# First products of three feed-forwards: seven half-size products of operand sums in place of eight

## What is computed

```python
def _swiglu(h, w_in, w_out):
    gu = h @ w_in
    return (jax.nn.silu(gu[..., :FFN_HIDDEN]) * gu[..., FFN_HIDDEN:]) @ w_out
```

## Time and profile before

| | us |
|---|---|
| three runs | 3299.5, 3304.2, 3306.3 |
| median | 3304.2 |
| span of the profiled execution (no other time is given for it) | 3302.2 |
| PE busy in it | 3203.2 |
| DVE busy | 1573.5 |
| ACT busy | 1129.4 |
| POOL busy | 417.1 |

### The profile page before, as it was taken

One profiled execution on the slowest core, in us unless ns is written; L12 is line 12 of the kernel. 1 busy time (PEld: TensorE's weight loads), 2 busy tenths in 40 slices (PEclk: granted clock), 3 DMA queues, 4 the chain that ended last, 5 costly groups with the idle time before them and its releaser, 6 DMA issues.

```text
span 3302.2 us, 45048 instructions
## 1 busy us (share of the span) xinstructions
PE 3203.2 (97%) x19414; PEld 2595.4 (79%) x19414; DVE 1573.5 (48%) x2498; ACT 1129.4 (34%) x1827; POOL 417.1 (13%) x622
## 2 busy tenths in 40 slices
PE   7999999999999999999999999999999999989999
PEld 5787888887887888887875677888887876668886
DVE  4646454446434654444246545343344437454544
ACT  6565532124434522223245443111112336431222
POOL 1302110002200300000010015000001311030000
PEclk9999999999999999999999999999999999999999
DMA  3111123223227322232243340222202222013221
GB/s 135 53 52 53 52 83 121 77 77 118 77 102 281 103 90 77 96 108 62 77 156 129 103 128 1 77 77 77 77 2 79 50 84 57 35 43 132 98 77 39
DMA packets 190743, 281.81 MB, mean 85 GB/s; under 512 B 19144, under 2 KB 122184, under 8 KB 190416
## 3 DMA queue, kind: packets, MB, share of 16 engines
q1 hardware_dynamic: 188368, 272.19, 24.8%
q10 hardware_dynamic: 2176, 6.73, 0.6%
HBM read 273.66 MB, written 2.10 MB: 84 GB/s over the span
## 4 chain that ended last, share of the span: by engine, by line
PE 90%; DVE 3%; ACT 3%; POOL 2%; issue 1%; DMA 1%; ACTq 0%; POOLq 0%; DVEq 0%; SPq 0%
PE ps L895 11%; PE ps L896 11%; PE ps L897 11%; PE ps L548 6%; PE ps L549 6%; PE ps L550 6%; PE ps L926 5%; PE ps L927 5%; PE ps L928 5%; PE ps L442 3%; PE ps L633 2%; PE ps L634 2%; PE ps L635 2%; PE ps L1533 2%; PE ps L1501 1%; PE ps L1709 1%
## 5 line engine op out<-in xcount | busy, mean ns | idle before, releaser
L451 ACT ACTIVATE R<-ring 128x2048 fp32r<-128x2048 f32 (+4 forms) x285 | 401.9, 1417 | 971.3 <-PE ps L928 345.0
L895 PE MATMUL ps<-R,R 128*128 128x512 f32 (+1 forms) x1760 | 654.3, 372 | 13.6 <-DVE R L810 8.6
L896 PE MATMUL ps<-R,R 128*128 128x512 f32 (+1 forms) x1760 | 650.3, 369 | 0.0
L897 PE MATMUL ps<-R,R 128*128 128x512 f32 (+1 forms) x1760 | 650.1, 369 | 0.0
L548 PE MATMUL ps<-R,R 128*128 128x512 f32 (+1 forms) x1016 | 395.9, 390 | 13.7 <-ACT U L451 4.0
L895 PEld LDWEIGHTS ps<-R,R 128*128 128x128 f32 x1760 | 333.2, 189 | 77.6 <-issue 13.0
L549 PE MATMUL ps<-R,R 128*128 128x512 f32 (+1 forms) x1016 | 379.2, 373 | 0.0
L550 PE MATMUL ps<-R,ringlo 128*128 128x512 f32 (+1 forms) x1016 | 378.4, 372 | 0.0
L897 PEld LDWEIGHTS ps<-R,R 128*128 128x128 f32 x1760 | 333.3, 189 | 56.2
L896 PEld LDWEIGHTS ps<-R,R 128*128 128x128 f32 x1760 | 333.4, 189 | 54.8 <-issue 0.5
L926 PE MATMUL ps<-R,R 128*128 128x512 f32 (+1 forms) x880 | 325.9, 370 | 0.9 <-DVE X L4029 0.9
(11 more groups left out here) (330 smaller groups left out, 4585.2 us busy)
## 6 DMA issues: line engine op xcount, KB each, us to landing
ring<-in_w_mod SPq DMA_DIRECT2D x24, 2048.0 KB, 9.8
ring<-in_ffn_w_in SPq DMA_DIRECT2D x44, 1024.0 KB, 11.9
ring<-in_w_ffn_in SPq DMA_DIRECT2D x44, 1024.0 KB, 12.2
ring<-in_ffn_w_out SPq DMA_DIRECT2D x10, 2048.0 KB, 8.0
ring<-in_w_ffn_out SPq DMA_DIRECT2D x10, 2048.0 KB, 8.0
ring<-in_dil_w_in SPq DMA_DIRECT2D x9, 2048.0 KB, 7.8
ring<-in_gdn_w_in SPq DMA_DIRECT2D x8, 2048.0 KB, 8.7
ring<-in_w_in SPq DMA_DIRECT2D x6, 1536.0 KB, 8.8
```

The source lines that it names most:

```text
L451: return act.e.activation(o, i, fn, **kw)
L895: pe.e.matmul(ps, w[0], x[0], start=(k == 0), stop=False)
L896: pe.e.matmul(ps, w[0], x[1], start=False, stop=False)
L897: t = pe.e.matmul(ps, w[1], x[0], start=False, stop=(k == 7))
```

## The change

In "ffn 0", "ffn 1" and ("ffn2", 1), that is the feed-forwards with the 512-token stream alone, the first product of the blocks from `FROM` on (2, 3 and 3, up to 10) is made by Winograd's form of Strassen's product. For one hidden tile (a unit) the weights are 2 x 2 quarters b11, b12, b21, b22 (half of the features; gate or up) and the activations a11 to a22 (half of the tokens; half of the features). Seven products of half the features and half the tokens (4 x 3 matmuls of 256 columns) give the four results. Their factors are sums of quarters, made by POOL for each unit (t1 to t4), and sums of activations ("shares" s1 to s4), made once by POOL and DVE before block `FROM`. All sums through products 1, 6, 7 and 4 run up in one PSUM bank "a"; ACT takes a snapshot of it after 1, 6 and 7 and the silu of it after 4. Products 2 and 5 have banks b and c. Four outputs of the block before stand inside each unit. Block 0 is made as before; blocks between are made plainly (`pe_in_plain`), with the high halves split by column into `NT`. The low halves are now written over the weights in the ring, so a slot of input weights is free when PE has read it, a block later, and one slot is kept for output weights, refilled by halves.

```diff
+        FROM = {"ffn 0": 2, "ffn 1": 3, ("ffn2", 1): 3}
...
+        PRODUCTS = {1: ("b11", "a11"), 2: ("b21", "a12"), 6: ("t2", "s2"), 5: ("t1", "s1"), 7: ("t3", "s3"),
+                    4: ("t4", "a22"), 3: ("b22", "s4")}
...
+            for c in range(2, 11):
+                if c < 10:
+                    w_in(c + 1)
+                sp.wait_ge(*at("down", tag, c - 2))
+                sp.wait_ge(*at("wo hi", tag, c - 1))
+                sp.e.dma_start(out_half(ring, tag, c), wo[256 * c:256 * c + 256, :].rearrange("(k p) n -> p k n", p=128)
+                               ).then_inc(*ring_filled[i].done("filled", (tag, "out", c)))
+            WSLOT.release((tag, "out", 0))
+            WSLOT.take_at([i], (tag, "out", 10))
+            if WSLOT.i % NS == i:
+                WSLOT.i += 1
...
+        def pe_unit(tag, c, j, between):
+
+            banks = {}
+            def product(i, x, first, last):
+                w, h = PRODUCTS[i]
+                if x not in banks:
+                    banks[x] = bank("sum", tag, c, j, x)
+                    PS.keep("sum", tag, c, j, x)
+                pe.wait_ge(*at("factor lo", tag, c, j, w))
+                if h in S_R:
+                    pe.wait_ge(*at("share lo", tag, h))
+                ps = banks[x][:, 0:256]
+                hi, lo = T_HI[w], factor(w, tag, c, j, True)
+                go_on = not first
+                for k in range(4):
+                    pe.e.matmul(ps, hi[:, k, :], share(h, 0)[:, k, :], start=(first and k == 0), stop=False, skip_group_check=go_on)
+                    pe.e.matmul(ps, hi[:, k, :], share(h, 1)[:, k, :], start=False, stop=False, skip_group_check=go_on)
+                    t = pe.e.matmul(ps, lo[:, k, :], share(h, 0)[:, k, :], start=False, stop=(k == 3), skip_group_check=go_on)
+                t.then_inc(*pe.done("unit", tag, c, j, i))
+                if last:
+                    PS.release("sum", tag, c, j, x)
+            product(1, "a", True, False)
+            product(2, "b", True, True)
+            pe.wait_ge(*at("snap", tag, c, j, 0))
+            product(6, "a", False, False)
+            product(5, "c", True, False)
+            pe.wait_ge(*at("snap", tag, c, j, 1))
+            product(7, "a", False, False)
+            between(0)
+            between(1)
+            pe.wait_ge(*at("snap", tag, c, j, 2))
+            product(4, "a", False, True)
+            pe.wait_ge(*at("up 2", tag, c, j))
+            product(3, "c", False, True)
+            between(2)
+            between(3)
+            if j:
+                pe.mark("gate up", tag, c)
+                pe.mark("ring read", (tag, "in", c))
+
+        def pe_out_one(tag, c, m, last):
+            ps = bank("product", tag, "out", c, m, 0)
+            pe.wait_ge(*at("wo lo", tag, c))
+            pe.wait_ge(*at("g lo", tag, c, 0, 1))
+            hi, lo = WOH[c == 10], out_half(ring_lo, tag, c)
...
+        def pe_ffn_s(tag, mid={}, between={}, last=None):
+            behind = (PS.i + 4) % 8
+            for c in range(12):
+                if c in mid:
+                    mid[c]()
+                if c == 0:
+                    pe_ffn_in(tag, [S], 0, between, 0)
+                elif c < FROM[tag]:
+                    pe_in_plain(tag, c)
+                elif c < 11:
+                    for j in range(2):
+                        pe_unit(tag, c, j, lambda i: pe_out_one(tag, c - 1, 4 * j + i, last))
+                    continue
+                if c:
+                    for m in range(8):
+                        pe_out_one(tag, c - 1, m, last)
...
+        def act_plain(tag, c, j):
+            for p in range(2):
+                act.wait_ge(*at("filled", (tag, "in", c)))
+                if c > 1:
+                    act.wait_ge(*at("product", "ffn", tag, c - 1, j, 0, 1))
+                elif j:
+                    act.wait_ge(*at("gate up", tag, 0))
+                activate(NT[j][p], column(ring, tag, c, j, p), ACT.Copy).then_inc(*act.done("plain hi", tag, c, j, p))
...
+        def act_out_hi(tag, c):
+            act.wait_ge(*at("filled", (tag, "out", c if c > 1 else 0)))
+            if c == 10:
+                act.wait_ge(*at("gate up", tag, 10))
+            elif c:
+                act.wait_ge(*at("down", tag, c - 1))
+            activate(WOH[c == 10], out_half(ring, tag, c), ACT.Copy).then_inc(*act.done("wo hi", tag, c))
...
+        def eng_shares(eng, tag, x):
+
+            f, tmp = S_F[x][1], S_F[x][0]
+            def then(o, a_, b_, op, *name):
+                eng.e.tensor_tensor(o, a_, b_, op).then_inc(*eng.done(*name))
+                eng.wait_ge(*at(*name))
+            eng.wait_ge(*at("x lo", (tag, 0), 7))
+            eng.wait_ge(*at("gate up", tag, 0))
+            if x in ("s1", "s3"):
+                one, two, op = ("a21", "a22", A_) if x == "s1" else ("a11", "a21", SUB)
+                then(f, share(one, 0), share(two, 0), op, "share part", tag, x, 0)
+                then(tmp, share(one, 1), share(two, 1), op, "share part", tag, x, 1)
+                then(f, f, tmp, A_, "share", tag, x)
+            elif x == "s2":
+                then(f, S_F["s1"][1], share("a11", 0), SUB, "share part", tag, x, 0)
+                then(f, f, share("a11", 1), SUB, "share", tag, x)
+            else:
+                then(f, share("a12", 0), S_F["s2"][1], SUB, "share part", tag, x, 0)
+                then(f, f, share("a12", 1), A_, "share", tag, x)
...
+        def pool_factors(tag, c, j):
+
+            def op(x, o, a_, b_):
+                pool.e.tensor_tensor(o, a_, b_, SUB).then_inc(*pool.done("factor", tag, c, j, x))
+            b11, b12, b21, b22 = (quarter(ring, tag, c, j, kh, p) for kh in range(2) for p in range(2))
+            t1, t2, t4 = (factor(x, tag, c, j, False) for x in ("t1", "t2", "t4"))
+            pool.wait_ge(*at("filled", (tag, "in", c)))
+            unit_free(pool, tag, c, j, 5)
+            op("t1", t1, b12, b11)
+            unit_free(pool, tag, c, j, 6)
+            pool.wait_ge(*at("factor", tag, c, j, "t1"))
+            op("t3", b12, b22, b12)
+            op("t2", t2, b22, t1)
+            pool.wait_ge(*at("factor", tag, c, j, "t2"))
+            op("t4", t4, b21, t2)
...
+        def act_unit(tag, c, j):
+            n = next_unit(c, j)
+            ps = PS.of("sum", tag, c, j, "a")[:, 0:256]
...
+            q, before = SQ.take("gate", tag, c, j, 0)
+            if before:
+                act.wait_ge(*at("sq read", *before))
+            g = TG.tiles[j]
+            snap(0, 1, q[:, HALF[0]])
+            hi("b11")
+            act.wait_ge(*at("tg read", tag, c - 1, j, 0))
+            snap(1, 6, g[:, HALF[0]])
+            hi("b21")
+            snap(2, 7, g[:, HALF[1]])
+            act.wait_ge(*at("gate 1", tag, c, j))
+            activate(q[:, HALF[0]], q[:, HALF[0]], ACT.Silu).then_inc(*act.done("silu 1", tag, c, j))
+            hi("t1", "t2")
+            act.wait_ge(*at("unit", tag, c, j, 4))
+            activate(q[:, HALF[1]], ps, ACT.Silu).then_inc(*act.done("ps", "sum", tag, c, j, "a"))
+            hi("t3", "t4", "b22")
...
+        def dve_unit(tag, c, j, take_out):
...
+            if c > FROM[tag] or j:
+                outs(*((c - 1, 2) if j else (c - 2, 6)))
+                dve_gate_lo(tag, *((c, 0) if j else (c - 1, 1)))
+                dve_factor(tag, c, j, "t4")
+                dve_factor(tag, c, j, "b22")
+            dve.wait_ge(*at("unit", tag, c, j, 2))
+            dve.wait_ge(*at("snap", tag, c, j, 0))
+            dve.e.tensor_tensor(q[:, HALF[0]], q[:, HALF[0]], b, A_).then_inc(*dve.done("ps", "sum", tag, c, j, "b"))
+            dve.mark("gate 1", tag, c, j)
+            if j == 0 and c > FROM[tag]:
+                dve_out_lo(tag, c - 1)
+            lo("b11")
+            dve.wait_ge(*at("snap", tag, c, j, 2))
+            dve.wait_ge(*at("unit", tag, c, j, 5))
+            dve.e.tensor_tensor(g[:, HALF[1]], g[:, HALF[1]], c_, A_).then_inc(*dve.done("up 2", tag, c, j))
+            outs(c - 1, 4 * j)
+            lo("t1", "b21", "t2")
+            dve.wait_ge(*at("unit", tag, c, j, 3))
+            dve.e.tensor_tensor(g[:, HALF[0]], g[:, HALF[0]], c_, A_).then_inc(*dve.done("ps", "sum", tag, c, j, "c"))
+            for x in (("ps", "sum", tag, c, j, "c"), ("ps", "sum", tag, c, j, "a"), ("silu 1", tag, c, j)):
+                dve.wait_ge(*at(*x))
+            dve.e.tensor_tensor(g, q[:, 0:512], g, M).then_inc(*dve.done("gate", tag, c, j))
+            dve.mark("sq read", "gate", tag, c, j, 0)
+            lo("t3")
+            if not n:
+                dve_gate_lo(tag, c, j)
+                outs(c - 1, 6)
...
+        def pool_unit(tag, c, j, mid={}):
+            n = next_unit(c, j)
+            if n:
+                pool_factors(tag, *n)
+            pool.wait_ge(*at("gate", tag, c, j))
+            pool.wait_ge(*at("down", tag, c - 2))
+            pool.e.tensor_copy(GR_[0][c % 2][0][:, j, :], TG.tiles[j]).then_inc(*pool.done("g hi", tag, c, j, 0))
```

(122 more changed lines are left out.)

181 lines of the change are left out of this document (168 added, 13 removed).

## The result

The change made the kernel slower: 3315.2 us median of 4 runs (3313.6 to 3322.9) against 3302.6 (3299.5 to 3306.3), ratio 1.0042 (95% 1.0027 to 1.0056). The forecast was 3310, range 3287 to 3333. The profiled execution of the changed kernel is the slowest of its four (3322.9; span 3320.8, against 3302.2 before), so its trace has 18.6 us to explain where the medians have 13. One execution of a kernel of the experiments, wo10_early, took 10889.6 us where its nine others took 3304.0 to 3311.9, and is left out of its comparison.

What follows compares the result with a forecast made beforehand. PE, busy 97% of the span, was taken as the bound. The terms -37.5 - 7.8 + 8 + 17 + 2.5 + 12 + 8.5 + 3 gave +5.7 us on 3302.2, or 3308; with the median 2 us higher, 3310, range 3287 to 3333.

Steps and rivals of the forecast that it cites:

- matmuls: First product of 25 blocks: 168 half-width matmuls for 96 full ones gain 1.5 us a block, 37.5 us in all.
- first unit, 2nd and 3rd: Second and third feed-forward: PE stands 4 us each for the first factor, queued on DVE behind evacuations and share splits; +8.
- first unit, 1st, with its clock: First feed-forward: PE waits 17 us for POOL's late shares, factors and casts, then 2.5 us for the lowered clock.
- last outputs: Block 10's output weights, split only after its last unit, hold PE: 4.5 us in the third feed-forward, 3.7 and 4.0 elsewhere; +12.
- side work, with its clock: Second feed-forward: other work delays snapshots in blocks 5 and 7 and output weights' splits in 9 and 10; +8.5 (4 to 12).
- start of the third: Third feed-forward: the 5.09 us wait for DVE's weight split and 2.5 us of lowered clock behind it go; -7.8.
- clock at the five gaps: Lowered PE clock after five pauses of 4 to 4.5 us: between 0 and 12 us, taken as +3.
- half-width price: A 256-column matmul costs 0.1198 us from start to start, by the profile's rows, against 0.2267 for 512 columns.
- POOL's chain in the first feed-forward: Ahead of the first unit, POOL's and DVE's work laid end to end puts POOL's last cast at 491, PE's start at 499.
- The rival with shorter stalls: POOL and DVE hinder less: first unit waits 7.5 us, side work costs 4, clock nothing; 3293, if that stall is under 10; chance 0.27.
- The rival with late units: A hand-over in each unit misses by 0.5 us, so 50 units cost 25 us: 3335; chance 0.2.

Runs made afterwards that it cites:

- wo10_early: Changed kernel with block 10's output weights split inside its last unit, after product 5, in all three feed-forwards; 3309.8 us, 1.0016 of the kernel before.
- plain_halves: Changed kernel with each 512-column matmul of the plain blocks' first product made as two of 256; 3326.5 us, 1.0074 of the kernel before.
- first_unit_order: Changed kernel with POOL's last cast ahead of the factors and DVE's share low halves and b11 ahead of the evacuations; 3308.3 us, 1.0017 of the kernel before.
- short_shares: Changed kernel with POOL's three shares in the first feed-forward made from high halves only, leaving work out; 3303.5 us, 1.0007 of the kernel before.
- from_3: Changed kernel with the first feed-forward's units starting at block 3 instead of 2; 3310.2 us, 1.0014 of the kernel before.
- second_column: Changed kernel with DVE making block 1's second-column low half ahead of a gate in the third feed-forward; 3315.5 us, 1.0039 of the kernel before.

## Why the prediction came out as it did

The time lies in the range and on the side to which I gave most (slower, 0.38, though hardly more than the 0.37 for no change). The terms of the sum, against the changed kernel's trace (excess of the distance from start to start over the price by width, which makes a wait some 0.16 us longer than the profile's; the cold matmuls in a row of their own except where said):

| step | forecast | measured |
|---|---|---|
| matmuls | -37.5 | -38.0 |
| first unit, 2nd and 3rd | +8 | +8.2 |
| first unit, 1st, with its clock | +19.5 | +16.3 |
| last outputs | +12 | +10.5 |
| side work, with its clock | +8.5 | +9.0 |
| start of the third | -7.8 | -0.3 |
| clock at the five gaps | +3 | +9.8 |
| plain blocks | none | +1.8 |
| sum | +5.7 | +17.3 |

That the time came out within 6 us of the forecast owes something to luck: the trace's sum is 11.6 above mine, and the profiled execution lies 7.7 above the median.

**Right.** The half-width price, 119.8 ns, held in 25 blocks and in plain_halves; the price of the Trainium skill (TensorE: Matmul & The Clock Gate, Back-to-back issue gap), which that section gives for a single matmul by itself, would have given 21 us more, and the trace is against it. No wait in a steady unit but where side work stands.

**POOL's chain in the first feed-forward: right in method, luckier in number.** The stall took 13.2 us in two pieces, for the 17: the outputs waited too, for a bank that DVE's late gate held. The chain ended at 490.95 for my 491, but this feed-forward began 2.2 us later than in the trace that I summed from (427.43 for 425.25). Timeline of POOL in the changed kernel:

```profile
456.88 5.20 POOL L1108 TENSOR_TENSOR U<-R 128x1024 f32<-128x1024 f32 x2
...
477.60 0.61 POOL L1443 CAST R<-U 128x512 fp32r<-128x512 f32 x1 [4.45 <-DVE U L1430]
```

From its first share at 456.88 POOL took 34.1 us, where laying both engines' work end to end gives 35.8. And I took the upper end "since POOL is never idle there": it stood idle for 4.45 of them, waiting for DVE's gate, while DVE was at its own share. The sum holds because DVE was then at work in its place.

**Last outputs: right in sum.** 13.6 of waits, 1.3 at the next stage, less 4.3 of waits and clock that the second feed-forward had there before and lost. By feed-forward that is 5.8, 0.3 and 4.5 for a forecast of 3.7, 4.0 and 4.5, so two misses cancel.

**Side work: near in size, in one place for a wrong reason.** My 8.5 had no clock in it; the waits themselves came to 7.1, the cold matmuls to 1.9. In blocks 9 and 10 I had the output weights' split late; PE waited 1.75 for a bank whose evacuation (L694) stood behind DVE's scaling. In block 7 I had 2.6 for 1.1.

**"The clock at the five gaps": mis-sized**, 3 for 9.8. I argued from a pause of 2.5 us that had kept the clock; every gap of 3.7 to 4.4 us brought it down, at 1.5 to 2.9 each. This and the next are the two steps that moved the sum, by 6.8 and 7.5 us the same way.

**"A gain at the start of the third": failed.** I followed the halves of the first column past the wait and had the second's "wanted 10.9 us later". The wait there was not one late split but POOL's residual work and DVE's splits taking turns; moving the splits only moved the place where PE met it. The experiments above show that it stays within 0.5 us over three orders; that taking work away would end it is argued, not tried.

The rival with shorter stalls (whose 7.5 should be 6.6 by the same sum: 480 + 4.9 + 3.7 - 482) failed with its condition: the first feed-forward's stall was not under 10. The rival with late units found none.

## What to carry to other kernels

Cost a restructured stage at its seams. Its steady blocks gave exactly what the counts said, and the seams (first unit, last outputs, alignment of banks, work hung in from elsewhere) took more than all of it back; mended, the same change was worth 0.9% the other way. Price a gap with its cold matmuls. Where a wait survives two changes of order, add up the work instead.

## What the hardware did that I had not expected

A short operation pays for a long one beside it. The changed kernel's timeline of DVE in block 1 of the first feed-forward, beside the POOL operations that begin at 456.88 (above):

```profile
456.95 2.88 DVE L1435 TENSOR_TENSOR R<-U,R 128x512 fp32r<-128x512 f32 x1 [0.71 <-POOL R L1443]
459.75 6.75 DVE L1088 TENSOR_TENSOR ringlo<-ring,R 128x1024 fp32r<-128x1024 f32 x2
```

0.69 us of work took 2.88, as it began 0.07 after an operation of POOL that took 2.40 and ended 0.55 after it; two subtractions of 1.2 took 6.75. The Trainium skill (SBUF — State Buffer, SBUF: two separate sides) says that whichever starts first holds the shared pair of ports for the whole instruction; the trace agrees. And the same short wait had cold matmuls behind it in some executions and not in others. The 2.07 us wait of block 5 of the second feed-forward was followed by 1.5 to 1.6 us of them, beginning 0.2 to 1.3 us after PE had started again, in the traces of the changed kernel, first_unit_order and wo10_early, and by 0.1 in those of short_shares, from_3, second_column and plain_halves. The 1.75 us wait of block 9 had 1.6 behind it in short_shares, from_3, second_column and first_unit_order, and 0.1 in the other three.
